# Modulation vectors of a two-block transformer kernel: weight panels multiplied and summed on GpSimd, partitions summed on TensorE

## What is computed

```
N_MOD = 9
mods = jnp.split((jax.nn.silu(c) @ w_mod[layer] + b_mod[layer])[:, None, :], N_MOD, axis=-1)
mods_c = jnp.split(jax.nn.silu(c_ctx) @ w_mod[layer] + b_mod[layer], N_MOD, axis=-1)
sh1, sc1, g1, sh2, sc2, g2, sh3, sc3, g3 = mods
sh1c, sc1c, g1c, sh2c, sc2c, g2c, sh3c, sc3c, g3c = mods_c
h = h + 0.5 * g1 * swiglu(modulate(h, norm_ffn1[layer], sh1, sc1), w_ffn1_in[layer], w_ffn1_out[layer])
```

## Time and profile before

| | us |
|---|---|
| time, median of 3 runs (3160.12 to 3161.12) | 3160.28 |
| the profiled execution's own time | 3162.73 |
| its span | 3160.9 |
| PE busy | 3088.8 (98%) |
| DVE busy | 1496.5 (47%) |
| ACT busy | 1012.7 (32%) |
| POOL busy | 247.7 (8%) |

### The profile page before, as it was taken

One profiled execution on the slowest core, in us unless ns is written; L12 is line 12 of the kernel. 1 busy time (PEld: TensorE's weight loads), 2 busy tenths in 40 slices (PEclk: granted clock), 3 DMA queues, 4 the chain that ended last, 5 costly groups with the idle time before them and its releaser, 6 DMA issues. The chain is left out here.

```text
span 3160.9 us, 35210 instructions
## 1 busy us (share of the span) xinstructions
PE 3088.8 (98%) x14974; PEld 2469.5 (78%) x14974; DVE 1496.5 (47%) x2276; ACT 1012.7 (32%) x1484; POOL 247.7 (8%) x190
## 2 busy tenths in 40 slices
PE   8999999999999999999999999999999999999998
PEld 6756778877666887878888888878787876778887
DVE  4566333344655334352222325566666775443333
ACT  4543222234533223242112124342323233332222
POOL 0233000011312000000000001010101012000000
PEclk9999999999999999999999999999999999999999
DMA  4114442222124422221211212121212123222222
GB/s 180 42 54 160 151 151 102 93 89 77 49 73 175 159 93 74 98 96 54 80 54 62 74 44 97 52 97 44 97 44 97 44 97 125 95 84 100 94 100 74
DMA packets 45212, 286.15 MB, mean 91 GB/s; under 512 B 5167, under 2 KB 5695, under 8 KB 19584
## 3 DMA queue, kind: packets, MB, share of 16 engines
q1 hardware_dynamic: 42480, 269.77, 24.1%
q0 software_dynamic: 2576, 14.14, 1.2%
HBM read 277.56 MB, written 6.32 MB: 90 GB/s over the span
## 5 line engine op out<-in xcount | busy, mean ns | idle before, releaser
L722 PE MATMUL ps<-A1h,whi 128*128 128x512 f32 x2336 | 931.1, 399 | 29.6 <-DVE wlo L1527 12.8
L723 PE MATMUL ps<-A1l,whi 128*128 128x512 f32 x2336 | 914.3, 391 | 0.0
L724 PE MATMUL ps<-A1h,wlo 128*128 128x512 f32 x2336 | 913.8, 391 | 0.0
L1527 DVE TENSOR_TENSOR wlo<-wraw,whi 128x2048 fp32r<-128x2048 f32 (+2 forms) x220 | 464.9, 2113 | 269.7 <-ACT whi L1106 269.5
L722 PEld LDWEIGHTS ps<-A1h,whi 128*128 128x128 f32 x2336 | 441.8, 189 | 129.6 <-issue 23.0
L1106 ACT ACTIVATE whi<-wraw 128x2048 fp32r<-128x2048 f32 (+2 forms) x220 | 383.2, 1742 | 472.7 <-PE ps L724 471.0
L724 PEld LDWEIGHTS ps<-A1h,wlo 128*128 128x128 f32 x2336 | 440.9, 189 | 93.1
L723 PEld LDWEIGHTS ps<-A1l,whi 128*128 128x128 f32 x2336 | 441.8, 189 | 89.1 <-issue 2.6
L1704 DVE TENSOR_TENSOR SIL<-SIL,ps 128x512 f32<-128x512 f32 (+1 forms) x110 | 69.8, 634 | 585.5 <-PE ps L724 504.5
L1268 ACT ACTIVATE SIL<-ps 128x512 f32<-128x512 f32 (+1 forms) x110 | 61.0, 554 | 713.2 <-PE ps L724 713.2
L1884 DVE SCALAR_TENSOR_TENSOR CA<-YIN,vec,CA 128x512 f32<-128x512 f32 x240 | 180.2, 751 | 7.3
(11 more groups left out here) (362 smaller groups left out, 4243.6 us busy)
## 6 DMA issues: line engine op xcount, KB each, us to landing
wraw<-wstream SPq DMA_DIRECT2D x159, 1024.0 KB, 4.8
MW<-wstream SPq DMA_DIRECT2D x36, 1024.0 KB, 5.1
wraw<-wstream SPq DMA_DIRECT2D x42, 768.0 KB, 4.3
wraw<-wstream SPq DMA_DIRECT2D x34, 640.0 KB, 3.9
wraw<-wstream SPq DMA_DIRECT2D x4, 960.0 KB, 4.6
hk<-gd POOLq DMA_DIRECT2D x1, 2560.0 KB, 15.4
X<-xT SPq DMA_DIRECT2D x4, 512.0 KB, 7.5
sx<-X POOLq DMA_DIRECT2D x1, 2048.0 KB, 6.6
```

The source lines that it names most:

```text
L722: mm(o, l[0], r[0], start=start, stop=False)
L723: mm(o, l[0], r[1], start=False, stop=False)
L724: return mm(o, l[1], r[0], start=False, stop=stop)
L1527: tt(wlo[i_ % 2][:, 0:n], wraw[i_ % 2][:, 0:n], raw(whi[i_ % 2][:, 0:n]), SUB).then_inc(ev("lo", i_).by(dve_wlo), 1)
```

## The change

The 36 panels are no longer multiplied on PE. POOL multiplies a panel by the condition, which it reads with a repeated index (128 x 2048), and then adds halves together three times (1024, 512 and 256 columns), so that 128 x 256 partial sums remain. Panels 0 to 19 are made for both conditions (eight operations), 20 to 35 for one (four). Layer 0 makes panels 0 to 11 and layer 1 panels 12 to 35, in one loop `mod_sums`, which stands on POOL between `restore` of ln1 and `add_up` of ln2. POOL loads its own panels (two buffers). PE then only sums the partitions: with the partial sums as weights and one column of ones, two matmuls for each panel and condition, four panels at a point, at nine points: behind gate panels 9 and 15 of f0 and at ln2; behind 9, 16, 19 (two groups) and 21 of f1 and at ln2. ACT's copies are gone, DVE adds the bias for eight columns at once. A panel from the ninth on also waits for PE's product of an earlier group, panels 28 to 35 for that of group 4 (behind gate panel 16 of f1).

```
-        m_landed = [count(f"m_landed{i}", 16) for i in range(3)]
+        m_landed = [count(f"m_landed{i}", 16) for i in range(2)]
...
+        BOTH = 5
+        MOD_PANELS = (range(0, 12), range(12, 36))
+        mod_groups = {("f0", 9): [0], ("f0", 15): [1], ("ln2", 0): [2],
+                      ("f1", 9): [3], ("f1", 16): [4], ("f1", 19): [5, 6], ("f1", 21): [7], ("ln2", 1): [8]}
...
             def mods(*point):
-                for what, m in mod_points[point]:
-                    if what == "make":
-                        b = AB.take("modp", m)
-                        e.wait_ge(b.before, ev("c32", int(m >= FIRST_MODS[1])), ev("mod landed", m))
-                        for k in range(8):
-                            c = 32 * (k % 4)
-                            last = mm(b.ap[c:c + 32, 0:256], c32[:, k, :], MW[m % 3][:, 256 * k:256 * k + 256], start=k < 4, stop=k > 3)
-                        last.then_inc(b.full.by(product), 1)
-                    elif what == "turn":
-                        b = AB.take("modt", m)
-                        e.wait_ge(b.before, ev("mrow", m), ev("vec"))
-                        for t in range(2):
-                            last = mm(b.ap[:, 2 * t:2 * t + 2], mrow[m % 2][:, 128 * t:128 * t + 128], v("sel", 0, 2), start=True, stop=True)
-                        last.then_inc(b.full.by(product), 1)
+
+                for i in mod_groups.get(point, ()):
+                    b = AB.take("mod", i)
+                    e.wait_ge(b.before, ev("mats"))
+                    for p in range(4):
+                        for who in range(2 if i < BOTH else 1):
+                            e.wait_ge(ev("mod sum", 4 * i + p, who))
+                            for t in range(2):
+                                at = 2 * (2 * p + t) + who
+                                last = mm(b.ap[:, at:at + 1], mod_sum(4 * i + p, who)[:, 128 * t:128 * t + 128], ones[:, 0:1], start=True, stop=True)
+                    last.then_inc(b.full.by(product), 1)
...
-                mods("ln1", l, 0)
                 squares(OB, SQA, ("ln1", l), 512, 8)
-                mods("ln1", l, 1)
...
-                mods("ln2", l, 0)
+                mods("ln2", l)
                 squares(OB, SQA, ("ln2", l), 512, 8)
-                mods("ln2", l, 1)
             gates("f2", "c", opC, 0)
             squares(OB, SQA, ("rms1",), 512, 8)
             gates("f2", "c", opC, 1)
-            mods("rms1")
...
+            def load_mod(m):
+                dma(MW[m % 2][:, :], bass.AP(a["wstream"].tensor, mod_at[m], [[2048, 128], [1, 2048]])).then_inc(
+                    ev("mod landed", m).by(m_landed[m % 2]), 16)
+
+            def mod_sums(panels):
+
+                for m in panels:
+                    w = MW[m % 2]
+                    e.wait_ge(ev("mod landed", m), AB.of("mod", (3 if m < 28 else 4) if m > 19 else m // 4 - 2).full if m > 7 else None)
+                    e.wait_ge(ev("mod sum", m - 1, 0) if m > panels[0] else None)
+                    made = [(w, 0)] if m >= 4 * BOTH else [(MP, 1), (w, 0)]
+                    for to, who in made:
+                        c = csv[:, :, who:who + 1].broadcast_to([128, 8, 256])
+                        tt(to[:, :].rearrange("p (k n) -> p k n", n=256), w[:, :].rearrange("p (k n) -> p k n", n=256), c, MUL).then_inc(
+                            ev("mod step", m, who, 2048).by(pool_mod), 1)
+                    for n in (1024, 512, 256):
+                        for to, who in made:
+                            e.wait_ge(ev("mod step", m, who, 2 * n))
+                            tt(to[:, 0:n] if n > 256 else mod_sum(m, who), to[:, 0:n], to[:, n:2 * n], ADD).then_inc(
+                                ev("mod step", m, who, n).by(pool_mod), 1)
+                    for to, who in made:
+                        ev("mod sum", m, who).same(ev("mod step", m, who, 256))
+                    if m + 2 in panels:
+                        e.wait_ge(ev("mod sum", m, 0))
+                        load_mod(m + 2)
...
                 attention(l)
+                e.wait_ge(ev("pv", l, "C", 2), ev("csil"))
+                for m in MOD_PANELS[l][:2]:
+                    load_mod(m)
                 add_up(TA[:, 3, :], X, ("ln1", l), lambda c: ev("x", "wo", l, c), ev("rs", "q", l))
...
                 restore(opN[l], ("ln1", l))
+                mod_sums(MOD_PANELS[l])
                 add_up(TA[:, 3, :], X, ("ln2", l), lambda c: ev("x", f"f{l}", 3, c), ev("rs", "c1") if l else ev("rs", "ln1", l))
```

More of the change, by code:

```diff
@@ L635, in width, with mod_sum @@
             return 128 * stream[i]["blocks"]
[L638 to L670 removed]
+        BOTH = 5
+        MOD_PANELS = (range(0, 12), range(12, 36))
+        mod_groups = {("f0", 9): [0], ("f0", 15): [1], ("ln2", 0): [2],
+                      ("f1", 9): [3], ("f1", 16): [4], ("f1", 19): [5, 6], ("f1", 21): [7], ("ln2", 1): [8]}
+        def mod_sum(m, who):
+            cells = macc[int(m in MOD_PANELS[1])]
+            return cells[m % 8][:, who, :] if m < 4 * BOTH else cells[(m // 2 - 6) % 8][:, m % 2, :]
         def mod_ready(i):
[L673 removed]
+            return [ev("mod", i)]
         def mod(i, c, who):
@@ L953, in gates, with ffn @@
                     used(p, b.full)
-            def ffn(name, streams, points=0, between=None, beside=None):
+            def ffn(name, streams, between=None, beside=None):
                 for g, js in enumerate(HIDDEN):
@@ L1110, in at @@
                 prep(index[key] + 1)
-            def mods(*point, part=None):
-                made = [x for x in mod_points[point] if x[0] == "row"]
-                for what, m in made if part is None else made[:1] if part == 0 else made[1:]:
-                    if what == "row":
-                        b = AB.of("modp", m)
-                        e.wait_ge(b.full, AB.of("modt", m - 2).full if m > 1 else None)
-                        act(mrow[m % 2][:, :], b.ap[:, 0:256], ACT.Copy, bias=0.0, scale=1.0).then_inc(ev("mrow", m).by(act_out), 1)
-                        b.free.same(ev("mrow", m))
             def high(op, k, src, group=0):
@@ L1255, in attention, with ffn @@
                         b.free.same(ev("vC", l, x[0]))
-            def ffn(name, streams, ring, points=0, between=None, last=None):
+            def ffn(name, streams, ring, between=None, last=None):
                 for g, js in enumerate(HIDDEN):
@@ L1532, in mods @@
             def mods(*point):
-                for what, m in mod_points[point]:
-                    if what == "turn":
-                        b = AB.of("modt", m)
-                        e.wait_ge(b.full, ev("vec"))
-                        for t in range(2):
-                            d = MOD[:, 4 * m + 2 * t:4 * m + 2 * t + 2]
-                            last = ts(d, b.ap[:, 2 * t:2 * t + 2], v("bmod", 2 * m + t), None, ADD)
-                        last.then_inc(ev("mod", m).by(dve_out), 1)
-                        b.free.same(ev("mod", m))
+                for i in mod_groups.get(point, ()):
+                    b, n = AB.of("mod", i), 2 if i < BOTH else 1
+                    e.wait_ge(b.full, ev("vec"))
+                    tt(MODv[:, i, :, 0:n], b.ap[:, 0:16].rearrange("p (c w) -> p c w", w=2)[:, :, 0:n],
+                       v("bmod", 8 * i, 8).unsqueeze(2).broadcast_to([128, 8, n]), ADD).then_inc(ev("mod", i).by(dve_out), 1)
+                    b.free.same(ev("mod", i))
             def low(op, k, src, group=0):
```

98 lines of the change are left out of this document (19 added, 79 removed).

## The result

The changed kernel takes **3287.7 us** at the median against 3160.7 in the same session: a ratio of 1.040 (95% interval 1.0386 to 1.0413), 127 us slower. The prediction said slower and 3221 (3180 to 3272), so the sign is right and the time lies above the range.

A forecast was written before the change was run, and what follows sets the result against it. PE, busy 98% of the span, was taken as the bound, with DVE's waits for POOL deciding: -32 - 12 + 22 + 25 + 56 + 2 = +61 us on 3160.3, so 3221 us, range 3180 to 3272.

The forecast's parts named there:

- the feed-forward panels: In f0 and f1, DVE waiting for POOL makes PE stop: 14 us and 11 us, bounds 5 and 45 together.
- the clock, taken as 2: PE runs at 1.2 GHz for a while behind the long stop at the context: +2 us.
- my rule: DVE and POOL share a port pair; whichever comes later waits until the other's current instruction has ended.
- The context: Behind f1's context, DVE's emissions and decays wait for POOL instructions, and PE stands idle: +56 us.
- The longer of the two sums: The context's cost if DVE operations with one SBUF input wait as well: 60 us, against 48 without them.
- What is removed: Modulation matmuls taken off PE in f0 and f1, 18 points at 1.69 us plus two starts: -32 us.
- the norms: Time won at ln1, ln2 and rms1 where panels and copies go: -12 us, bounds -6 and -16.
- What PE gets: PE's new groups of small one-column matmuls, 4.0 us for both conditions, 2.0 single: +22 us, up to +34.
- What POOL gets: POOL's panels, 4.7 us per 2048-column product: 230 us of work in layer 0, 312 in layer 1 within 339.
- POOL is late at ln2 of layer 1: Rival: POOL's panels end too late, so ln2's `add_up` and PE's total wait; about 3290 us, chance 0.13.
- the waits were not small: Rival "The waits are small": DVE gets through without waiting for POOL's wide instructions; about 3140 us, chance 0.10.
- the context was spared only in part: Rival: only the panels stop, and DVE's chain at the context takes turns more favourably with POOL; 3188 us, chance 0.12.

The follow-up runs named there:

- the kernel with one gap: The changed kernel plus one gap in each panel for both conditions, between POOL's first and second product; 3198.3 us, ratio 1.0116.
- the run with the last addition alone: The changed kernel with only the 256-column addition left of POOL's work in each panel (wrong vectors); 3152.8 us, ratio 0.9972.
- the last version: The changed kernel plus first-product gaps, panels 0 to 15 in layer 0, POOL's pause ahead of panel 29, moved groups, spread small matmuls; 3140.6 us, ratio 0.9932.

## Why the prediction was wrong

**The step that failed is the reading of the earlier trace rows**, that "the later one waits until the other's current instruction has ended". It holds where POOL's operations have a gap between them or no load ahead of them, and was drawn from `restore`, eight operations without a load among them. The panels for both conditions have both a load and no gap, and there the wait goes to the panel's end (in ten of 16; in the others POOL had itself waited for DVE first). The term "the feed-forward panels", 14 us in f0 and 11 in f1, was 60 and 39 us of stops in the changed kernel (of f1's 62 us, 22 are behind the context and 1 was there before), and the clock, taken as 2, cost 15 in each (the rows of small matmuls included). In the world of my rule, that of the kernel with one gap, the stops of the feed-forward panels are 2 us in either stage. So the term was wrong twice: too large for the rule, since two waits of under 4 us nearly always fit into the slack, and far too small for what happened.

**The context.** The mechanism was right, the size was not: with POOL at work the decays and emissions cost 46.2 us. I had 56. The count of operations was nearly right: the rows have 43 where I had 40, and 6.9 of them went by per panel (58.1 us, panels of 9.3) where I let 6 go by, which gave 60 us from the first to the last; the measured 58.1 lies beside it. The step that failed here is the next one, "It comes out whole as idle time of PE": DVE needs 12.1 us for these operations without POOL too, and those were in the old time already. 58 less 12 is the 46 that was measured. Nor does nearly each operation wait: 25 of the 43 take longer than without POOL, while 25 POOL operations go by. (The longer of the two sums, 60, lies 4 us above the 56 taken, not 7 as the prediction has it.) The question left open about operations with one SBUF input is answered: they wait. But in the changed kernel the stop was only 22.0 us, 17.5 more than before. DVE's last emissions met POOL, its decays did not: POOL had got to the panels that wait for group 4, and PE, 124 us later than in the kernel before, had not made it. The last of the decays' operations took 0.17 us each, which the prediction had named as what would prove it wrong. What that refutes here is only that POOL was at work beside them.

**What is removed, and the norms.** -32 and -12 held: f0's work is 10 us less (-19.5 and +8 had been said), f1's 1 more (-13 and +14); ln1 gave 1.4 twice, as said, ln2 with rms1 8.8 where 8 were taken.

**What PE gets.** A group was 4.12 us and a single one 1.7, as said (4.0 and 2.0). Missing was the clock behind a row of small matmuls. By the run with the last addition alone (a gain of 9 where 22 were forecast) the term is about +35 instead of +22; the clock behind the groups of f0 and f1 takes 12 us in that run.

**What POOL gets.** The wide product took 3.62 us, not 4.7, undisturbed; the additions 2.39, 1.29 and 0.73. The group of the products in the changed kernel:

```profile
L2064 POOL TENSOR_TENSOR MW<-MW,small 128x2048 f32<-128x2048 f32 x36 | 141.8, 3940 | 76.4 <-PE ps L749 76.0
```

So POOL waited 76 us for PE's groups and was never late; its last panel ended at 1463, and ln2's `add_up` began at 1476 when DVE had its input. The rival "POOL is late at ln2 of layer 1" had 3290 us, next to the measured time, but its mechanism didn't occur, and the two numbers met by chance. The other rivals fell too: the waits were not small, and the context was spared only in part and for another reason.

**The sum, redone** for the kernel with one gap: 3160 - 32 - 12 + 35 (groups with the clock) + 3 (feed-forward panels) + 43 (context, by its stop) + 2 = 3199; measured 3198.3. The +35 and the +43 are measured in these experiments and not forecast. The changed kernel has 89 us more from the shut-out, in which is counted that the context gets shorter. That the load and the missing gap together make the shut-out is shown by taking away either; why they do, inside POOL, stays a reading.

## What to carry to other kernels

Where VectorE works on two SBUF inputs beside GpSimd, let GpSimd wait for its own operation once behind every DMA that it issues, and never run a row of operations behind a load without a gap; that is nearly free and was worth 89 to 110 us here. A chain of small VectorE operations pays about one wait for each GpSimd operation that goes by (46 us for 43 operations here), so halt GpSimd there if it has time to spare. When you forecast such a chain, take off what it costs without GpSimd. Spread small matmuls over a stream of wide ones, or put them where TensorE waits anyway.

## What the runs showed that I had not expected

- Behind a load issued by GpSimd, a VectorE operation with two SBUF inputs was shut out for up to eight GpSimd operations (15.9 us), and let in by the first gap of 0.07 us, or once a GpSimd operation had itself waited for VectorE. An operation that arrives during the issue itself (0.59 us) is passed by the next one too.
- A busy GpSimd costs next to nothing when it lets VectorE in: in the last version it is busy for 350 of f0's 374 us, and the stops there are 4 us.
- A row of 16 one-column float32 matmuls (32 records), 4.1 us with no stop, is followed by the clock at 1.2 GHz for some 6 us; spread out, the clock stays at 2.4 GHz.
- A product whose second input is read with a repeated index took 3.62 us for 2048 columns, 1.77 ns a column, where an addition takes 2.39 for 1024.
- VectorE operations of one SBUF input and 8 columns wait for GpSimd as well (L1715: 4.10 us instead of 0.17).
